# Two transformer-like blocks on one core: projections in three 256-column passes, and a new distance between weight and input addresses

## What is computed

```
h += rglru_mixer(rmsnorm(h))         # u = h @ w_in (1024x3072), conv, gates, scan; (rec * y) @ w_out (1536x1024)
h += swiglu(rmsnorm(h))              # u = h @ w_gu (1024x5632); (silu(g) * v) @ w_down (2816x1024)
h += nsa_mixer(...) ; h += swiglu(...) ; h = rmsnorm(h)
h += 0.5 * swiglu_2(...)
h += s5_mixer(...)                   # ... g * sigmoid(g @ w_glu); @ w_out (1024x1024)
h += 0.5 * swiglu_2(...) ; h += 0.5 * swiglu_2(...)
h += moba_mixer(...)                 # @ w_qkv, attention, @ w_out (1024x1024)
h += 0.5 * swiglu_2(...)
```

## The kernel before

| buffer | before | after |
|---|---|---|
| hg_hi, hg_lo, hid (both parts), hq, mo_o, glu | 224 | 224 |
| rec (both parts) | 320 | 320 |
| w_hi0, w_lo0 | 256 | 288 |
| w_hi1, w_lo1 | 288 | 288 |
| w_hi2, w_lo2 | 320 | 288 |
| w_hi3, w_lo3 | 352 | 288 |

## Time and profile before

### The profile page before, as it was taken

How to read it: one execution, slowest core, us unless ns; L and a number is a source line. 1 busy time by engine, 2 the same in 40 slices (tenths; PEclk the granted TensorE clock), 3 DMA queues, 4 the chain that set the end, 5 groups by cost and what they waited for, 6 DMA issues and landing times.

```text
span 1705.7 us, 31820 instructions
## 1 busy us (share of the span) xinstructions
PE 1677.9 (98%) x12958; PEld 1576.4 (92%) x12958; DVE 1265.5 (74%) x1657; ACT 832.6 (49%) x1104; POOL 375.4 (22%) x425
## 2 busy tenths in 40 slices
PE   7999999999999999999999999999999999999999
PEld 7789998898789999899989999998999999899998
DVE  7898889785868988788857866666666665676663
ACT  5865444343665444454444255444444445554442
POOL 0223012535505132610032130002100137330000
PEclk9999999999999999999999999999999999999999
DMA  8245567675206788555646445564455544335560
GB/s 321 107 141 211 210 219 262 232 281 190 77 2 205 244 267 300 183 191 194 228 166 235 137 162 177 193 220 176 152 193 204 215 150 168 125 126 198 202 230 33
DMA packets 50711, 321.02 MB, mean 188 GB/s; under 512 B 7696, under 2 KB 8912, under 8 KB 20144
## 3 DMA queue, kind: packets, MB, share of 16 engines
q1 hardware_dynamic: 36432, 280.61, 46.1%
q0 software_dynamic: 12736, 36.87, 6.7%
q10 hardware_dynamic: 1440, 2.10, 0.3%
HBM read 307.39 MB, written 10.09 MB: 186 GB/s over the span
## 4 chain that ended last, share of the span: by engine, by line
PE 87%; DVE 8%; ACT 2%; issue 2%; DMA 1%; POOL 0%; ACTq 0%; DVEq 0%; POOLq 0%
PE bank L2268 18%; PE bank L2262 17%; PE bank L2263 16%; PE bank L2264 16%; PE bank L2269 9%; DVE w_lo L1436 2%; PE bank L2549 1%; PE bank L2916 1%; PE bank L2868 1%; ACT w_hi L1006 1%; PE bank L2734 1%; PE bank L2623 1%; PE bank L2454 1%; PE bank L2559 1%; DVE rstd L1446 1%
## 5 line engine op out<-in xcount | busy, mean ns | idle before, releaser
L1436 DVE TENSOR_TENSOR w_lo<-raw,w_hi 128x1024 fp32r<-128x1024 f32 (+2 forms) x486 | 644.8, 1330 | 259.1 <-ACT w_hi L1006 257.9
L1006 ACT ACTIVATE w_hi<-raw 128x1024 fp32r<-128x1024 f32 (+2 forms) x486 | 538.2, 1117 | 546.7 <-PE bank L2264 323.0
L2262 PE MATMUL bank<-hg_hi,w_hi 128*128 128x256 f32 x2648 | 748.1, 283 | 12.3 <-DVE hg_lo L1441 10.4
L2263 PE MATMUL bank<-hg_lo,w_hi 128*128 128x256 f32 x2648 | 743.6, 281 | 0.0
L2264 PE MATMUL bank<-hg_hi,w_lo 128*128 128x256 f32 x2648 | 742.7, 280 | 0.0
L2262 PEld LDWEIGHTS bank<-hg_hi,w_hi 128*128 128x128 f32 x2648 | 500.6, 189 | 17.6 <-DVE w_lo L1436 11.5
L2264 PEld LDWEIGHTS bank<-hg_hi,w_lo 128*128 128x128 f32 x2648 | 501.1, 189 | 0.0
L2263 PEld LDWEIGHTS bank<-hg_lo,w_hi 128*128 128x128 f32 x2648 | 500.7, 189 | 0.2
L2268 PE MATMUL bank<-hid,w_hi 128*128 128x512 f32 x1056 | 370.2, 394 | 0.0
L2269 PE MATMUL bank<-hid,w_lo 128*128 128x256 f32 x1056 | 296.5, 281 | 0.0
L2268 PEld LDWEIGHTS bank<-hid,w_hi 128*128 128x128 f32 x1056 | 198.3, 188 | 46.4 <-issue 0.8
(11 more groups left out here) (412 smaller groups left out, 1900.3 us busy)
## 6 DMA issues: line engine op xcount, KB each, us to landing
raw<-in_w SPq DMA_DIRECT2D x189, 1024.0 KB, 4.8
raw<-in_w SPq DMA_DIRECT2D x48, 1408.0 KB, 6.5
raw<-in_w SPq DMA_DIRECT2D x8, 768.0 KB, 4.8
b_rows<-in_s_b_rows POOLq DMA_DIRECT2D x8, 512.0 KB, 8.0
l_rows<-s_powers POOLq DMA_DIRECT2D x64, 64.0 KB, 10.6
s_ca<-cp_s POOLq DMA_DIRECT2D x8, 512.0 KB, 4.6
s_ba<-ba_s POOLq DMA_DIRECT2D x8, 512.0 KB, 8.0
ba_slot<-s_ba POOLq DMA_DIRECT2D x8, 512.0 KB, 5.3
```

The lines of the kernel that those rows point to most:

```text
L1006: act.activation(w_hi[s][:, 0:n], raw[r][:, c * n:(c + 1) * n], ACT.Copy).then_inc(hi_made, 1)
L1436: dve.tensor_tensor(w_lo[s][:, 0:n], raw[r][:, c * n:(c + 1) * n], w_hi[s][:, 0:n].bitcast(F32), ALU.subtract).then_inc(lo_made, 1)
L2262: pe.matmul(psum, w_hi_ap, x_hi_ap, start=first, stop=False, **kw)
L2263: pe.matmul(psum, w_hi_ap, x_lo_ap, start=False, stop=False, **kw)
```

## The change

All calls of wide_passes become calls of three_passes with 256 columns in place; wide_passes is gone. VectorE adds only the bank's first half to h. Two gaps of 32 and 96 bytes are put before and behind the weight slots, and the 32 bytes at the end of each w_lo go, so that all eight slot buffers come to lie at 288.

```diff
--- before.py
+++ after.py
@@ -189,10 +189,11 @@
         raw = [sb(f"raw{r}", [P, UNIT_MAX]) for r in range(RAW)]
         mask_s = sb("mask_s", [P, T + P], F32R, at=place[0] - (T + P) * 4)
         eps = sb("eps", [P, 1])
+        place[0] += 32
         w_hi, w_lo = [], []
         for s in range(SPLIT):
             w_hi.append(sb(f"w_hi{s}", [P, UNIT_MAX // 2], F32R))
-            w_lo.append(sb(f"w_lo{s}", [P, UNIT_MAX // 2 + 8], F32R))
+            w_lo.append(sb(f"w_lo{s}", [P, UNIT_MAX // 2], F32R))
         vec = sb("vec", [P, NVEC])
         ones_d = sb("ones_d", [P, P])
         sumsq = sb("sumsq", [P, T])
@@ -208,6 +209,7 @@
         joint = sb("joint", [P, 24])
         joint_gain, joint_scale, eps_2 = joint[:, 0:8], joint[:, 8:16], joint[:, 16:17]
 
+        place[0] += 96
         region = (place[0], nc.sbuf_usable_end // 32 * 32)
         ffn = Region(*region)
         hid = ffn.sb("hid", [P, 2, FT * T], F32R)
@@ -231,7 +233,6 @@
         first_half_in = sem("first_half_in")
         squares_made = sem("squares_made")
         pool_const = sem("pool_const")
-        h_half = sem("h_half")
         h_written = sem("h_written")
         hghi_made = sem("hghi_made")
         hg_made = sem("hg_made")
@@ -1461,8 +1462,6 @@
                     dve.scalar_tensor_tensor(h[:, m, :], h[:, m, :], gain("final", m), joint_rstd[:, :],
                                              ALU.mult, ALU.mult).then_inc(h_written, 1)
 
-            halves_added = [0]
-
             def twice(row):
 
                 return row[:, None, :].broadcast_to([P, 2, T])
@@ -1470,16 +1469,9 @@
             def two(x):
                 return x.rearrange("p (a t) -> p a t", a=2)
 
-            def add_to_h(ph, m, psum, parts=2):
-
-                if parts == 1:
-                    dve.scalar_tensor_tensor(h[:, m, :], psum[:, 0:T], ph["scale"], h[:, m, :], ALU.mult, ALU.add).then_inc(h_written, 1)
-                    return
-                dve.scalar_tensor_tensor(h[:, m, :], psum[:, T:2 * T], ph["scale"], h[:, m, :], ALU.mult, ALU.add).then_inc(h_half, 1)
-                halves_added[0] += 1
-                dve.wait_ge(h_half, halves_added[0])
-                dve.scalar_tensor_tensor(h[:, m, :], psum[:, 0:T], ph["scale"], h[:, m, :], ALU.mult, ALU.add)\
-                   .then_inc(h_written, 1)
+            def add_to_h(ph, m, psum):
+
+                dve.scalar_tensor_tensor(h[:, m, :], psum[:, 0:T], ph["scale"], h[:, m, :], ALU.mult, ALU.add).then_inc(h_written, 1)
 
             def project(ph, half0, per_tile, banks=(2, 3)):
                 for m in range(KT):
@@ -1488,7 +1480,7 @@
                     if per_tile == 2 and (m or not plain):
                         split_lo(half + SPLIT)
                     dve.wait_ge(half_used, half + per_tile)
-                    add_to_h(ph, m, bank[banks[m % len(banks)]], 1 if plain else 2)
+                    add_to_h(ph, m, bank[banks[m % len(banks)]])
                     if m or per_tile == 1 or not plain:
                         split_lo(half + per_tile - 1 + SPLIT)
                     if ph["next"]:
@@ -2263,11 +2255,6 @@
                 pe.matmul(psum, w_hi_ap, x_lo_ap, start=False, stop=False, **kw)
                 return pe.matmul(psum, w_lo_ap, x_hi_ap, start=False, stop=last, **kw)
 
-            def wide_passes(psum, w_hi_ap, w_lo_ap, x_pair, first, last):
-
-                pe.matmul(psum[:, :].rearrange("p (a t) -> p a t", a=2), w_hi_ap, x_pair, start=first, stop=False)
-                return pe.matmul(psum[:, 0:T], w_lo_ap, x_pair[:, 0, :], start=False, stop=last)
-
             def weights(half, it=0):
 
                 pe.wait_ge(lo_made, n_split(half) + 2 * BODY * it)
@@ -2334,8 +2321,8 @@
                         for q in range(per_half):
                             if m == first:
                                 ready(k)
-                            last = wide_passes(bank[2 + m % 2], hi[:, q * P:(q + 1) * P], lo[:, q * P:(q + 1) * P],
-                                               x[:, :, k, :], k == 0, k == halves * per_half - 1)
+                            last = three_passes(bank[2 + m % 2][:, 0:T], hi[:, q * P:(q + 1) * P], lo[:, q * P:(q + 1) * P],
+                                               x[:, 0, k, :], x[:, 1, k, :], k == 0, k == halves * per_half - 1)
                             k += 1
                         last.then_inc(half_used, 1)
 
@@ -2385,8 +2372,8 @@
                             k = j * (FT // 2) + q
                             if m == 0 and k % 2 == 0:
                                 pe.wait_ge(hid_made, pairs0 + k // 2 + 1)
-                            last = wide_passes(bank[2 + m % 2], hi[:, q * P:(q + 1) * P], lo[:, q * P:(q + 1) * P],
-                                               hid[:, :, k * T:(k + 1) * T], k == 0, k == FT - 1)
+                            last = three_passes(bank[2 + m % 2][:, 0:T], hi[:, q * P:(q + 1) * P], lo[:, q * P:(q + 1) * P],
+                                               hid_hi[:, k * T:(k + 1) * T], hid_lo[:, k * T:(k + 1) * T], k == 0, k == FT - 1)
                         last.then_inc(half_used, 1)
 
                 if ph["prep"] is not None:
@@ -2462,7 +2449,7 @@
                             w = slice(k % 6 * P, k % 6 * P + P)
                             if m == 2:
                                 pe.wait_ge(rec_made, k // GT + 1)
-                            last = wide_passes(bank[REC_BANKS[m % 2]], hi[:, w], lo[:, w], rec[:, :, k, :], k == 0, k == RT - 1)
+                            last = three_passes(bank[REC_BANKS[m % 2]][:, 0:T], hi[:, w], lo[:, w], rec_hi[:, k, :], rec_lo[:, k, :], k == 0, k == RT - 1)
                         if used:
                             last.then_inc(half_used, used)
 
@@ -2522,8 +2509,8 @@
                     for k in ks:
                         if m == 0:
                             pe.wait_ge(o_made, self.jobs + 2 * (k // self.per_group) + 2)
-                        last = wide_passes(bank[ATT_BANKS[m]], hi[:, k * P:(k + 1) * P], lo[:, k * P:(k + 1) * P],
-                                           self.x[:, :, k, :], k == 0, k == KT - 1)
+                        last = three_passes(bank[ATT_BANKS[m]][:, 0:T], hi[:, k * P:(k + 1) * P], lo[:, k * P:(k + 1) * P],
+                                           self.x[:, 0, k, :], self.x[:, 1, k, :], k == 0, k == KT - 1)
                     if k == KT - 1:
                         last.then_inc(half_used, 1)
```

## The result

| | before | after |
|---|---|---|
| median of the runs compared, us | 1707.3 (4 runs, 1705.3 to 1711.6) | 1682.8 (4 runs, 1675.6 to 1691.4) |
| ratio after / before | | 0.9858 [0.9835, 0.9881] |
| profiled execution, us | 1707.6 | 1686.8 |
| span, us | 1705.7 | 1685.0 |
| PE busy / not busy in the span, us | 1677.9 / 27.8 | 1652.6 / 32.4 |

The change makes the kernel faster by 1.4%. The forecast was 1664.5 us; the result is 18 us more. It lies in the range, near its upper end, beside the 1686.5 us of rival A in half of the matmuls. The four runs of after lie 16 us apart, those of before 6 us.

What follows compares the result with a forecast made beforehand. TensorE bounds the kernel: number of matmuls times the distance between their starts. Terms -32.1 - 9.7 + 0.5 - 1.1 - 0.5 + 1.1 = -41.8 us against the 1706.4 us median gave 1664.5 us, range 1658 to 1688.

Steps and rivals of the forecast that it cites:

- rival A: Slow pattern persists at slot 1's distance, 117.5 ns a matmul: in half 1686.5 us, chance 0.11; everywhere 1708.5 us, 0.07.
- the main forecast: Whole kernel: every slot takes slot 1's fast period of 113.8 ns a matmul, giving 1664.5 us; chance 0.68.
- What bounds the kernel: From about 20 us on, time is the number of matmuls times the distance between neighbouring starts; PE busy 98%.
- Rival B: Something other than addresses sets slot 1 apart; only the third matmul's cost remains: 1710.9 us, chance 0.06.
- Item 1: Existing three-pass products: 117.7 to 113.8 ns a matmul, 3.9 ns less on 8232 matmuls, -32.1 us.
- Item 2: Wide products become three passes: 349.3 to 341.4 ns on 1232 products, -9.7 us; far end 353.1 ns.
- Item 3: The recurrence's 72 products stay 32 bytes past the slots and take 356.4 ns each, +0.5 us.
- Item 4: Token-major products, weights and inputs exchanged: 3.9 ns less on each of 288 matmuls, -1.1 us.
- Item 5: Adding to h: VectorE loses one of two additions in 76 tiles; only the program's end gains, -0.5 us.
- Item 6: Gain given back to VectorE and GpSimd waits in the recurrence phase, +1.1 us; weight transfers costed at nothing.
- Rival C: VectorE becomes the bound in the two FFN phases preparing S5 weights; 10.6 us missing, 1675 us; chance 0.08.

Runs made afterwards that it cites:

- the mixed pairs: Two kernels with w_hi and w_lo at different distances from the inputs, another pair for each slot: 1717.7 and 1716.4 us, one run each.
- the added products: The changed kernel plus a 256-column float32 product behind each of eight K products and at two other breaks: 1673.4 us, 0.9805 of before.
- after again: The changed kernel run anew with no edit, for a second profile: 1678.7 us (5 runs), 0.9827 of before.

## Why the prediction was right or wrong

The sign and the cause were right; of the expected 42 us a good half came. The range held the result because its upper part was drawn for rival A, to which I had given 0.11, and it is A in about half of the matmuls that came; the main forecast, with 0.68, did not.

- **What bounds the kernel**: right. PE is busy 98% of the span after as before, and nearly every change of the time is a change of the distance between starts; the place at 682 us (3.9 us) is the exception.
- **The addresses are the cause**: shown, by the addresses alone (0.9876), by their absence (1.0017, no fast window), by 96 bytes and by the mixed pairs. Rival B is out.
- **Item 1, -32.1 us, came to -21.6.** This is the step that was wrong: the term took 113.8 ns for every matmul, and the mean was 115.02. I took the period of slot 1 as the period of the distance, but it was the period of the distance *and* of having been entered afresh: before, every half in slot 1 was entered from a half at another distance. The kernel with slot 0 at 32 bytes bears this out: slot 1 behind it was fast in 55 of 60 halves, and in 41 of 60 with all slots alike. With all slots alike a stage is entered once and keeps what it got. Rival A said so in as many words. I gave it 0.11 for a half, because every re-entry that I had looked at behind a break was fast; those were few, and the earlier trace rows was the counter-example, which I put down to a single place.
- **Item 2, -9.7 us, came to about -5.3** with hq, mo_o and glu. Its near end, 341.4 ns, is right in the fast rhythm (340.1 with the added products), its far end, 353.1, in the slow (353.2 with the old addresses). I had two ends and the truth was both, in turn.
- **Item 3**: rec took 350.1 ns, not 356.4. It gained 0.1 us where I gave 0.5 back, since before it took 351.5 ns and not the 349.3 of hid. In after again it took 3 x 117.8. That it misses the fast rhythm for its address is shown by its move to 64 bytes.
- **Item 4, -1.1 us**: token-major stayed at 117.8 ns in after, -0.1 us. It can be fast: with the added products its first 72 matmuls take 113.3 ns. glu stayed slow in every trace with all slots at 64 bytes and three passes: 353.4, 4.0 ns above before. Why glu never enters the fast rhythm is open.
- **Item 5**: right, 0.46 us at the end. VectorE did 32.0 us less, which gained nothing elsewhere.
- **Item 6, +1.1 us**: PE's time without work grew by 4.6 us, of which 2.3 are waits for w_lo and 2.3 the two waits at 682 us, in the middle of a down-projection; the clock took 1.6 us more behind them. I had costed all transfers at nothing, and from a single stage: the 56% stands in no line of the earlier trace rows, which give 0.57 for the plain stage and 0.79 for one that also prepares S5. A transfer of S5's data that came late is what this execution paid for.
- **Rival C**: not seen in the way it was put. In the two preparing phases the stretches alternate with 18.30 us of VectorE in a fast one and 17.77 in a slow one. TensorE did wait for VectorE once there, but VectorE had been idle for a DMA and not too busy.
- **The rule of the Trainium skill** on the read ports ("SBUF — State Buffer", section "Who interferes with whom") is not borne out here, if it is read as saying that TensorE's own two reads cannot disturb each other: by it the old and the new addresses had to give the same time with three passes, and they give 1.0017 and 0.9858. That the distance acts through these reads is not shown.

Open is what state decides at a break. Shown: the rhythm is kept over the stretch; a wait of equal length can end either way; K products turn it over (31 of 32); with a 256-column float32 product behind them a fast rhythm stays fast (16 of 16), with a 128-column one it does not. Not shown: where the state lives. Open is also what exactly counts in the addresses. No run moved weights and inputs together, so the distance and the two positions, 224 and 288, are not told apart; rec, moved to 224, became fast as either would have it. That 512 is the period is not shown either: all tiles of a buffer have the same rest modulo 512, and a smaller period would fit as well. Distances over 128 bytes were not tried.

## What to carry to other kernels

Where TensorE issues matmuls of 256 columns back to back, read the distance between starts in the timeline, slot by slot, before looking for idle time: a busy share of 98% had nearly 4% in it. Put weights and inputs at one distance modulo 512, found by measuring each, since here 64 bytes is the only one of those tried that allows 113.3 ns; then count matmuls in equal windows, for such a rhythm holds or fails per stretch, and one execution shows one draw of it. Look at the granted clock in short windows behind each long wait, for 3.4 us at half the clock do not show in 40 slices. A period seen in one place is a forecast for others only if they are also *entered* in the same way.

## What the runs showed of the hardware

- Period of a 256-column float32r matmul by distance of weights and inputs modulo 512: 113.3 or 117.8 ns at 64 bytes, 118.2 to 118.6 at 32 (rec 116.7 or 117.8), 117 to 120 at 96, 118.3 at 128 (slot 3 of before), 119.6 at 0. With only one of the two weight tiles at 64 bytes it is 117.8 at best.
- At 64 bytes both rhythms are steady, for up to 1583 matmuls, at a granted clock of 1.00, and either occurs at DMA shares of 0.61 as well as of 0.97 and above, and with VectorE busy for 17 or 18 of 20 us. What changes them is a break of TensorE, down to a delay of 0.04 us, or products of another kind.
- One program spreads over 21 us in nine runs; between its two traced executions the rhythm makes 8.7 of 10.2 us. The version with the added products spreads over 5.
- Behind waits of 1.21 and 1.13 us, 2 us apart, the granted clock was 0.50 for 3.4 us in after; 15 matmuls of 256 columns then took 3.37 us instead of 1.77.
- A 512-column matmul takes 231.4 ns at the old addresses and 235.0 at 64 bytes: the distance that is best for one shape is not for another.
